# Products on half the partitions, issued alternately, and an attention output product on two column groups

## The chip, the cores and the metric

One core of a Trainium2 chip runs the whole kernel. The metric is device time in microseconds (us); lower is better. The time before is the median of three runs. The trace is of one more execution.

## What is computed

A trunk of two layers over 512 tokens of width 1024. The first layer mixes with sliding-window attention (8 query heads of 64, 2 key heads, window 128, a sink per head) and mLSTM (4 heads, chunks of 128). The second mixes with SSD (8 heads, chunks of 128, 2 groups) and an RWKV-7 recurrence (8 heads of 64). Each mixer is followed by a squared-ReLU MLP of width 4096. Cut to the parts that the change touches:

```python
o = jnp.einsum('bhgnqk,bnkhd->bnqhgd', p.astype(v.dtype), vb)          # attention's output product
qk = jnp.einsum('bnthd,bnshd->bntsh', qc, kc) * w_intra                # mLSTM
a_cum = jnp.cumsum((dt * A.astype(F32)).reshape(bsz, nc, L, G, hg), axis=2)
seg = a_cum[:, :, :, None] - a_cum[:, :, None, :]                      # SSD: every pair of rows in a chunk
decay = jnp.exp(jnp.where(causal, seg, -jnp.inf))
S = S * w_t[:, :, None, :] - sa[..., None] * b_t[:, :, None, :] + v_t[..., None] * k_t[:, :, None, :]   # RWKV-7
```

## The kernel before

Everything is written by hand per engine, with semaphores. The order of TensorE's work is a generator's: `even_front` and `odd_front` mix slots of the input projection (24 one-pass products of 512 columns each: high and low parts of weights and activations, L859 to L861) with the mixers' own small products; `rwkv_chunks` orders the last part of layer 1, where no projection is left to mix in. PSUM has eight banks. `make_plan` hands them out in turn in the order of use: a product may start once the one eight places before it in that order has been drained (`free`), and whoever reads it waits for `full`; `close` signals it.

Weights come by DMA in pieces; ScalarE writes the high part (L1371), GpSimd the low part (L768), and TensorE waits for the low part by `w_cut`. ScalarE cuts a piece only when its place in its queue comes.

The products of the change. Features lie on partitions, two heads of 64 in each block of 128, so a product of one head reads partitions 0 to 63 or 64 to 127 (`par`).

- `score` (L1017): for each of 8 units u, two heads of `par` 0 into one bank, then two of `par` 1 into another; VectorE and ScalarE make the softmax, `att_turn` turns it, and `att_out` (L1028) multiplies it by v two units later. v stands twice side by side (`v_dup`, written by four ScalarE copies, L1533), so that the result of 128 rows by 512 columns holds every head in both halves of the partitions; ScalarE's two drains (L1557) take the right quarter of it each.
- `qk_st` (L1056) and `inter` (L1081) of mLSTM: as the scores, two and two.
- `sub` (L1147): RWKV's blocks for the substitution, for each f four products of `par` 0, then four of `par` 1.
- `a_row` in `ssd_front` (L1168, L1172): for each half, a mask into the whole bank by one product, then four products over 32 partitions that add a row of `a_cum` to it. `a_turned` holds `a_cum` turned, on 32 partitions.
- `mats` (L1232 to L1235): for each of 8 heads four products of 128 columns into a bank, which VectorE masks and copies (`masked`, L2462). For the next chunk the heads' products stand between this chunk's: head 0 before `y`, head 1 before `s_rw` (L1326, L1327), heads 2 to 7 behind it. VectorE masks heads 0 and 1, takes `s_rw` (L2545, L2547), makes the new state (L2550), and masks the other six; `pt` (L1249) of the next chunk waits for all eight. Before the last chunk the turned `y_ssm` go between.

An fp32 product is two instructions in the trace.

Of the kernel before, what the change touches and what calls it, by code (L numbers as in the profile page):

```python
# [34 lines left out]
P = 128  # L35
T = 512
NT = T // P
# [185 lines left out]
def rwkv_chunks():  # L223

    def heads(n, first, last):
        for hh in range(first, last):
            yield "mats", n, hh // 2, hh % 2

    yield from heads(0, 0, 8)
# [4 lines left out]
    for n in range(NT):  # L234
# [53 lines left out]
def make_plan():  # L288
# [11 lines left out]
    for layer in range(2):  # L300
# [38 lines left out]
        else:  # L339
# [27 lines left out]
            for item in rwkv_chunks():  # L367
                put(*item)
# [16 lines left out]
def trunk(nc, dram, out):  # L385
    PLAN = make_plan()
    with ExitStack() as ctx:
# [182 lines left out]
        v_dup = take(NT + 1, 2, P)  # L570
# [90 lines left out]
        acum = tiny(2, 32)  # L661
# [174 lines left out]
        def _(pe):  # L836
# [141 lines left out]
            def even():  # L978
                dup = even_const("dup").rearrange("p (g m) -> p g m", g=2)
                turned = 0  # L980
                for item in even_front():
# [23 lines left out]
                    elif kind == "score":  # L1005
# [7 lines left out]
                        for par in range(2):  # L1013
                            o = free(pe, "score", u, par)
                            r = slice(64 * par, 64 * par + 64)
                            for a in range(2):
                                ins = mm(o[:, a * 256:(a + 1) * 256], q_rot[r, 2 * g + a, n * P:(n + 1) * P],  # L1017
                                         k_dup[r, g, n * P:n * P + 256], start=True, stop=True)
                            close(ins, "score", u, par)
# [30 lines left out]
                for n in range(NT):  # L1050
                    tok = slice(n * P, (n + 1) * P)
                    for par in range(2):
                        o = free(pe, "qk_st", n, par)
                        r = slice(64 * par, 64 * par + 64)
                        for a in range(2):
                            ins = mm(o[:, a * P:(a + 1) * P], conv_out[r, 2 + a, tok], conv_out[r, a, tok],  # L1056
                                     start=True, stop=True)
                        close(ins, "qk_st", n, par)
# [16 lines left out]
                    if n:  # L1075
                        pe.wait_ge(S["c_ready"], n)
                        for par in range(2):
                            o = free(pe, "inter", n, par)
                            r = slice(64 * par, 64 * par + 64)
                            for a in range(2):  # L1080
                                ins = mm(o[:, a * 129:(a + 1) * 129], conv_out[r, a, tok], c_state[r, n, a, :],  # L1081
# [1513 lines left out]
```

## Time and profile before

| | |
|---|---|
| median of 3 runs | 1432.07 us (1429.0 to 1435.8) |
| profiled execution: its time | 1429.38 us |
| its span, first to last instruction | 1427.5 us |
| granted TensorE clock, mean | 0.970 |
| TensorE busy | 1352.4 us (95%) |
| GpSimd, VectorE, ScalarE busy | 657.1, 582.6, 535.6 us |

Busy time says how long an engine has at least one instruction at work. The chain follows the work that ended last back from the end. In a timeline a row may merge several instructions of a line; its second column reaches from the first one's start to the last one's end.

### The profile page before, as it was taken

How to read it: one execution, taken by the hardware profiler on the slowest of the kernel's cores; microseconds unless marked ns; L12 is line 12 of the kernel's file. 1: busy time of each engine (PE TensorE's matmuls, PEld its weight loads, DVE VectorE, ACT ScalarE, POOL GpSimd, SP SyncE). 2: the span in 40 equal slices, each digit the busy share in tenths (PEclk: the TensorE clock that was granted, in tenths of full speed). 3: DMA queues.
4: the chain of work that ended last, by engine and by line, in shares of the span. 5: the costliest groups of instructions: out<-in, count | busy, mean ns of one | idle time of the engine just before them, and what ended most of it. 6: DMA issues, size and time to landing. Idle time of an engine off the chain costs nothing.

```text
span 1427.5 us, 17763 instructions
## 1 busy us (share of the span) xinstructions
PE 1352.4 (95%) x6427; PEld 1085.4 (76%) x6427; DVE 582.6 (41%) x957; ACT 535.6 (38%) x871; POOL 657.1 (46%) x810
## 2 busy tenths in 40 slices
PE   5999968999999999999798999998999999999998
PEld 4777656788888888887477777888878888888886
DVE  4537667421221212345588567365442122121233
ACT  5345653341322413436553424533333132232332
POOL 4653213564554555664234432311365555564562
PEclk9999978999999999999899999999899999999999
DMA  8322101333323323332212211000133333323321
GB/s 271 89 74 60 60 1 31 103 89 91 102 89 89 102 88 93 98 89 74 59 45 67 79 48 30 1 2 1 45 89 90 103 89 92 100 88 95 97 89 59
DMA packets 198034, 109.12 MB, mean 76 GB/s; under 512 B 4570, under 2 KB 195280, under 8 KB 197840
## 3 DMA queue, kind: packets, MB, share of 16 engines
q1 hardware_dynamic: 197552, 108.16, 26.0%
q8 instruction: 43, 0.70, 0.2%
q14 instruction: 23, 0.19, 0.0%
q0 software_dynamic: 416, 0.07, 0.0%
HBM read 106.11 MB, written 2.10 MB: 76 GB/s over the span
## 4 chain that ended last, share of the span: by engine, by line
PE 73%; DVE 7%; ACT 3%; issue 2%; POOL 0%; DVEq 0%; ACTq 0%; POOLq 0%
PE ps L859 20%; PE ps L860 20%; PE ps L861 20%; PE ps L846 1%; PE ps L900 1%; PE ps L901 1%; PE ps L902 1%; DVE late L2462 1%; PE ps L1263 1%; PE ps L1274 1%; PE ps L1252 1%; PE ps L1137 1%; PE ps L1249 0%; PE ps L1317 0%; DVE arena L2533 0%
## 5 line engine op out<-in xcount | busy, mean ns | idle before, releaser
L768 POOL TENSOR_TENSOR w_lo<-raw_w,w_hi 128x256 fp32r<-128x256 f32 x760 | 613.3, 839 | 632.8 <-ACT w_hi L1371 632.8
L1371 ACT ACTIVATE w_hi<-raw_w 128x1024 fp32r<-128x1024 f32 x190 | 201.1, 1058 | 559.0 <-PE ps L861 441.0
L859 PE MATMUL ps<-hn_hi,w_hi 128*128 128x512 f32 x880 | 360.1, 409 | 9.6 <-POOL w_lo L768 8.8
L860 PE MATMUL ps<-hn_lo,w_hi 128*128 128x512 f32 x880 | 351.7, 400 | 0.0
L861 PE MATMUL ps<-hn_hi,w_lo 128*128 128x512 f32 x880 | 351.5, 399 | 0.0
L859 PE MATMUL ps<-hid_hi,w_hi 128*128 128x512 f32 x576 | 228.4, 397 | 0.0
L861 PE MATMUL ps<-hid_hi,w_lo 128*128 128x512 f32 x576 | 228.4, 396 | 0.0
L860 PE MATMUL ps<-hid_lo,w_hi 128*128 128x512 f32 x576 | 228.3, 396 | 0.0
L859 PEld LDWEIGHTS ps<-hn_hi,w_hi 128*128 128x128 f32 x880 | 167.6, 190 | 59.6 <-issue 17.9
L860 PEld LDWEIGHTS ps<-hn_lo,w_hi 128*128 128x128 f32 x880 | 167.9, 191 | 42.2 <-issue 3.1
L861 PEld LDWEIGHTS ps<-hn_hi,w_lo 128*128 128x128 f32 x880 | 167.6, 190 | 41.0
L1892 DVE TENSOR_TENSOR h<-h,ps 128x512 f32<-128x512 f32 x64 | 44.0, 688 | 259.2 <-PE ps L861 259.2
L859 PEld LDWEIGHTS ps<-hid_hi,w_hi 128*128 128x128 f32 x576 | 108.5, 188 | 26.4
L861 PEld LDWEIGHTS ps<-hid_hi,w_lo 128*128 128x128 f32 x576 | 108.5, 188 | 26.5
L860 PEld LDWEIGHTS ps<-hid_lo,w_hi 128*128 128x128 f32 x576 | 108.5, 188 | 26.4
L1881 DVE SCALAR_TENSOR_TENSOR relu<-ps,rms 128x512 f32<-128x512 f32 x64 | 44.3, 692 | 161.5 <-PE ps L861 160.7
L1884 DVE TENSOR_TENSOR hid_lo<-relu,hid_hi 128x512 fp32r<-128x512 f32 x64 | 53.7, 840 | 102.2 <-ACT hid_hi L1442 102.2
L1365 ACT ACTIVATE arena<-ps 128x512 f32<-128x512 f32 (+1 forms) x42 | 23.0, 575 | 56.2 <-PE ps L1317 23.2
L1440 ACT ACTIVATE relu<-relu 128x512 f32<-128x512 f32 x64 | 39.4, 616 | 10.0 <-DVE relu L1881 10.0
L1442 ACT ACTIVATE hid_hi<-relu 128x512 fp32r<-128x512 f32 x64 | 40.5, 633 | 2.0
L1365 ACT ACTIVATE rwkv_raw<-ps 128x512 f32<-128x512 f32 (+1 forms) x29 | 15.2, 540 | 50.4 <-PE ps L861 41.7
L2230 DVE TENSOR_TENSOR relu<-ps,rms 128x512 f32<-128x512 f32 x22 | 15.0, 684 | 40.2 <-PE ps L861 39.8
(371 smaller groups left out, 1444.5 us busy)
## 6 DMA issues: line engine op xcount, KB each, us to landing
raw_w<-in_w_up SPq DMA_DIRECT2D x64, 512.0 KB, 4.0
raw_w<-in_w_down SPq DMA_DIRECT2D x64, 512.0 KB, 3.6
raw_w<-in_o_w_in SPq DMA_DIRECT2D x27, 512.0 KB, 3.8
raw_w<-in_e_w_in SPq DMA_DIRECT2D x19, 512.0 KB, 3.8
raw_w<-in_e_w_out SPq DMA_DIRECT2D x8, 512.0 KB, 3.6
raw_w<-in_o_w_out SPq DMA_DIRECT2D x8, 512.0 KB, 3.5
rwkv_raw<-in_x SPq DMA_DIRECT2D x4, 512.0 KB, 8.4
out<-arena SPq DMA_DIRECT2D x8, 256.0 KB, 2.9
```

Source lines behind the costliest of these rows:

```text
L768: nc.gpsimd.tensor_tensor(w_lo[:, n % CUT, ks], raw_w[:, n % RING, ks], w_hi[:, n % CUT, ks].bitcast(F32), ALU.subtract).then_inc(w_cut, 1)
L859: mm(o, a_hi, b_hi, start=(k == 0), stop=False)
L860: mm(o, a_hi, b_lo, start=False, stop=False)
L861: ins = mm(o, a_lo, b_hi, start=False, stop=(k == KT - 1))
L1365: A(dst, o if src is None else src, ACT.Copy, scale=scale).then_inc(free_sem(*key), 1)
L1371: A(w_hi[:, n % CUT], raw_w[:, n % RING], ACT.Copy).then_inc(w_high, 1)
L1440: A(relu_t[:, j % 2, :], relu_t[:, j % 2, :], ACT.Square).then_inc(hid_square, 1)
L1442: A(hid_hi[:, j, :], relu_t[:, j % 2, :], ACT.Copy).then_inc(hid_high, 1)
L1881: V.scalar_tensor_tensor(out=relu_t[:, j % 2, :], in0=ps[:, b, :], scalar=0.0, in1=rms_t, op0=ALU.max, op1=ALU.mult).then_inc(bank_free[b], 1)
L1884: V.tensor_tensor(hid_lo[:, j, :], relu_t[:, j % 2, :], hid_hi[:, j, :].bitcast(F32), ALU.subtract).then_inc(hid_ready, 1)
L1892: V.tensor_tensor(h[:, j, :], h[:, j, :], ps[:, b, :], ALU.add).then_inc(bank_free[b], 1)
L2230: V.tensor_tensor(stage[:, i % 2, 3:3 + T], o, rms_t, ALU.mult).then_inc(free_sem(*key), 1)
```

## The change

The products that read half the partitions are issued in alternation: one of the lower half, one of the upper, each half into its own bank. That holds for `score`, `qk_st`, `inter`, `sub` and `mats`; `rwkv_chunks` now hands out `mats` by pairs of heads, the first pair before `y`. `a_row` needs the turned `a_cum` on partitions 0 to 31 and again on 32 to 63, so `a_cum` is made twice (one product more, `acum` of three parts) and turned with 64 columns; both masks go first, then the small products of the two halves in alternation. `att_out` keeps v once (`v_kept`) and makes the two `par` as products of 64 output rows each, into partitions 0 to 63 and 64 to 127 of one bank, so that one ScalarE drain takes both.

```diff
-    def heads(n, first, last):
-        for hh in range(first, last):
-            yield "mats", n, hh // 2, hh % 2
+    def pairs(n, first, last):
+        for f in range(first, last):
+            yield "mats", n, f
...
         if more:
-            yield from heads(n + 1, 0, 1)
+            yield from pairs(n + 1, 0, 1)
         yield "y", n
         if more:
-            yield from heads(n + 1, 1, 2)
             yield "s_rw", n
-            yield from heads(n + 1, 2, 8)
+            yield from pairs(n + 1, 1, 4)
...
-        v_dup = take(NT + 1, 2, P)
+        v_kept = take(NT + 1, 2, 64)
...
-        acum = tiny(2, 32)
+        acum = tiny(3, 32)
...
-                        for par in range(2):
-                            o = free(pe, "score", u, par)
-                            r = slice(64 * par, 64 * par + 64)
-                            for a in range(2):
-                                ins = mm(o[:, a * 256:(a + 1) * 256], q_rot[r, 2 * g + a, n * P:(n + 1) * P],
+                        o = [free(pe, "score", u, par) for par in range(2)]
+                        for a in range(2):
+                            for par in range(2):
+                                r = slice(64 * par, 64 * par + 64)
+                                ins = mm(o[par][:, a * 256:(a + 1) * 256], q_rot[r, 2 * g + a, n * P:(n + 1) * P],
                                          k_dup[r, g, n * P:n * P + 256], start=True, stop=True)
...
-                            ins = mm(o, v_dup[:, n + blk, g, :], att_pt[:, u % 2, blk, :],
-                                     start=(blk == 0), stop=(blk == 1))
+                            for par in range(2):
+                                ins = mm(o[64 * par:64 * par + 64, 0:256], v_kept[:, n + blk, g, :],
+                                         att_pt[:, u % 2, blk, par * 256:(par + 1) * 256],
+                                         start=(blk == 0), stop=(blk == 1))
...
-                        mm(o[:, 0:32], upper, da_, start=True, stop=True)
-                        close(mm(o[:, 32:64], ones, da_, start=True, stop=True), "a_cum")
+                        for twin in range(2):
+                            mm(o[:, 32 * twin:32 * twin + 32], upper, da_, start=True, stop=True)
+                        close(mm(o[:, 64:96], ones, da_, start=True, stop=True), "a_cum")
...
-                        for par in range(2):
-                            r = slice(64 * par, 64 * par + 64)
-                            o = free(pe, "sub", f, par)
-                            for t in range(NT):
-                                c = slice(t * P, (t + 1) * P)
-                                ins = mm(o[:, c], kk_s[r, f, c], b_s[r, f, c], start=True, stop=True)
-                            close(ins, "sub", f, par)
+                        o = [free(pe, "sub", f, par) for par in range(2)]
+                        for t in range(NT):
+                            c = slice(t * P, (t + 1) * P)
+                            for par in range(2):
+                                r = slice(64 * par, 64 * par + 64)
+                                ins = mm(o[par][:, c], kk_s[r, f, c], b_s[r, f, c], start=True, stop=True)
+                                if t == NT - 1:
+                                    close(ins, "sub", f, par)
...
+                        o = [free(pe, "a_row", n, half) for half in range(2)]
                         for half in range(2):
-                            o = free(pe, "a_row", n, half)
-                            mm(o.rearrange("p (a t) -> p a t", a=4), mask_r[:, 0:P], over(mask_r[:, P:2 * P], 1, 4),
-                               start=True, stop=False, skip_group_check=True)
-                            for j in range(4):
-                                c = 8 * n + 4 * half + j
-                                ins = mm(o[:, j * P:(j + 1) * P], ident[0:32, c:c + 1].to_broadcast([32, P]),
-                                         a_turned[0:32, :], start=False, stop=True, skip_group_check=True)
-                            close(ins, "a_row", n, half)
+                            mm(o[half].rearrange("p (a t) -> p a t", a=4), mask_r[:, 0:P],
+                               over(mask_r[:, P:2 * P], 1, 4), start=True, stop=False, skip_group_check=True)
+                        for j in range(4):
+                            for half in range(2):
+                                r = slice(32 * half, 32 * half + 32)
+                                c = 32 * half + 8 * n + 4 * half + j
+                                ins = mm(o[half][:, j * P:(j + 1) * P], ident[r, c:c + 1].to_broadcast([32, P]),
+                                         a_turned[r, :], start=False, stop=True, skip_group_check=True)
+                                if j == 3:
+                                    close(ins, "a_row", n, half)
...
-                    for par in range(2):
-                        r = slice(64 * par, 64 * par + 64)
-                        ins = A(y_mix[r, 2 * g:2 * g + 2, n * P:(n + 1) * P],
-                                o[r, par * 256:par * 256 + 256].rearrange("p (a t) -> p a t", a=2), ACT.Copy)
-                    ins.then_inc(free_sem("att", u), 1)
+                    A(y_mix[:, 2 * g:2 * g + 2, n * P:(n + 1) * P], o[:, 0:256].rearrange("p (a t) -> p a t", a=2),
+                      ACT.Copy).then_inc(free_sem("att", u), 1)
```

`qk_st`, `inter` and `mats` are rewritten in the same way; the four copies of v are one.

TensorE, in `rwkv_chunks`, from the end of `y` (L1315, L1317) of chunk 0 over `s_rw` (L1326, L1327); before:

```order
L1315 MATMUL ps<-rwkv_raw,late 128x64
L1317 MATMUL ps<-arena,late 128x64
L1232 MATMUL ps<-arena 128x128
L1233 MATMUL ps<-arena,rwkv_raw 128x128
L1234 MATMUL ps<-rwkv_raw 128x128
L1235 MATMUL ps<-rwkv_raw,arena 128x128
L1326 MATMUL ps<-rwkv_raw,arena 128x128
L1327 MATMUL ps<-arena 128x128
```

The same place now (`y` is L1330 and L1332, `s_rw` L1341 and L1342, `mats` L1248):

```order
L1330 MATMUL ps<-rwkv_raw,late 128x64
L1332 MATMUL ps<-arena,late 128x64
L1341 MATMUL ps<-rwkv_raw,arena 128x128
L1342 MATMUL ps<-arena 128x128
L1341 MATMUL ps<-rwkv_raw,arena 128x128
L1342 MATMUL ps<-arena 128x128
L1341 MATMUL ps<-rwkv_raw,arena 128x128
L1342 MATMUL ps<-arena 128x128
L1341 MATMUL ps<-rwkv_raw,arena 128x128
L1342 MATMUL ps<-arena 128x128
L1248 MATMUL ps<-arena 128x128 x2
L1248 MATMUL ps<-arena,rwkv_raw 128x128 x2
```

Head 1's four products have gone from between `y` and `s_rw` to before `y`; the other heads follow `s_rw` in pairs.

TensorE, in `ssd_front` of chunk 0, between b's turns (L846) and `cb` (L1177); before:

```order
L846 MATMUL ps<-main,arena 128x128 x2
L1168 MATMUL ps<-mask_r 128x512
L1172 MATMUL ps<-arena,main 128x128 x4
L1168 MATMUL ps<-mask_r 128x512
L1172 MATMUL ps<-arena,main 128x128 x4
L1177 MATMUL ps<-arena 128x128 x2
```

And now:

```order
L849 MATMUL ps<-main,arena 128x128 x2
L1178 MATMUL ps<-mask_r 128x512 x2
L1184 MATMUL ps<-arena,main 128x128 x8
L1190 MATMUL ps<-arena 128x128 x2
```

The second mask stands directly behind the first, and the eight small products are in one row.

## Rows read from the trace of the kernel before

**Rows 1.** The page: PE's busy time, and the chain's shares by engine.

```profile
PE 1352.4 (95%) x6427; PEld 1085.4 (76%) x6427; DVE 582.6 (41%) x957; ACT 535.6 (38%) x871; POOL 657.1 (46%) x810
...
PE 73%; DVE 7%; ACT 3%; issue 2%; POOL 0%; DVEq 0%; ACTq 0%; POOLq 0%
```

**Rows 2.** Busy time by stage: stretch, its length, busy time (instructions) by engine, clock.

```profile
95.00:175.00 80.00, 78.95 (x372) 56.59 (x371) 53.84 (x110) 45.25 (x119) 27.05 (x36) 1.00 0.20 60
...
875.00:1002.00 127.00, 112.83 (x936) 104.17 (x936) 62.64 (x115) 52.33 (x103) 25.14 (x22) 0.94 0.00 1
```

**Rows 3.** Timeline of PE, LoRA products: start, length, engine, line, shape [idle before].

```profile
656.72 0.69 PE L1114 MATMUL ps<-rwkv_raw,lora 64*128 64x512 f32 x1
656.72 0.69 PE L1116 MATMUL ps<-rwkv_raw,lora 64*128 64x512 f32 x1
```

**Rows 4.** Timeline of PE, scores of one unit and what follows.

```profile
118.59 1.14 PE L1017 MATMUL ps<-arena,rwkv_raw 64*128 64x256 f32 x8
119.67 0.33 PE L846 MATMUL ps<-main,rwkv_raw 128*128 128x128 f32 x1
```

**Rows 5.** Timeline of PE, one attention output product and what follows.

```profile
129.60 1.88 PE L1028 MATMUL ps<-y_mix,arena 128*128 128x512 f32 x4
131.32 0.59 PE L1042 MATMUL ps<-arena,main 128*128 128x512 f32 x1
```

**Rows 6.** Timeline of PE, a_row of chunk 1 and what follows.

```profile
816.89 0.48 PE L1168 MATMUL ps<-mask_r 128*128 128x512 f32 x1
817.30 1.15 PE L1172 MATMUL ps<-arena,main 32*128 32x128 f32 x8
818.39 0.50 PE L1168 MATMUL ps<-mask_r 128*128 128x512 f32 x1
...
819.90 0.71 PE L1177 MATMUL ps<-arena 128*128 128x128 f32 x4
```

**Rows 7.** Timeline of ScalarE and of VectorE, end of attention.

```profile
178.58 0.77 ACT L1557 ACTIVATE y_mix<-ps 64x256 f32<-64x256 f32 x2 [0.46 <-PE ps L1028]
...
188.21 2.20 DVE L2101 SCALAR_TENSOR_TENSOR arena<-rwkv_raw,small 128x128 f32<-128x128 f32 x8 [4.64 <-ACT rwkv_raw L1365]
```

**Rows 8.** Timeline of PE, sub of f = 0, projections, and the wait behind f = 3.

```profile
716.60 1.71 PE L1147 MATMUL ps<-arena 64*128 64x128 f32 x16
718.24 0.50 PE L859 MATMUL ps<-hn_hi,w_hi 128*128 128x512 f32 x1
718.58 0.40 PE L860 MATMUL ps<-hn_lo,w_hi 128*128 128x512 f32 x1
718.81 0.40 PE L861 MATMUL ps<-hn_hi,w_lo 128*128 128x512 f32 x1
...
742.74 0.47 PE L859 MATMUL ps<-hn_hi,w_hi 128*128 128x512 f32 x1 [2.61 <-POOL w_lo L768]
```

**Rows 9.** The chain (start, length, what), before the RWKV chunks.

```profile
874.47 0.70 DVE late L2462
```

**Rows 10.** Timeline of PE and of VectorE, from y to s_rw of chunk 0.

```profile
907.70 0.48 PE L1232 MATMUL ps<-arena 64*128 64x128 f32 x2
...
908.79 0.49 PE L1326 MATMUL ps<-rwkv_raw,arena 128*128 128x128 f32 x2
...
910.87 0.69 DVE L2547 COPY arena<-ps 128x512 f32<-128x512 f32 x1 [1.29 <-PE ps L1327]
```

**Rows 11.** The chain in chunk 1, the group norm.

```profile
934.67 6.29 DVE arena L2533 x6
```

**Rows 12.** Timeline of VectorE between chunks 2 and 3.

```profile
975.60 3.68 DVE L2462 SCALAR_TENSOR_TENSOR late<-ps,main 128x512 f32<-128x512 f32 x6 [0.15 <-DVE arena L2550]
979.67 1.53 DVE L1848 TENSOR_TENSOR hid_lo<-ps,hid_hi 128x512 fp32r<-128x512 f32 x2 [0.40 <-ACT hid_hi L1783]
```

**Rows 13.** PE by stretch, before and in pt: length, busy (count), granted clock, DMA.

```profile
914.70:917.30 2.60, 0.00 (x0) 1.00 0.00 0
917.40:920.80 3.40, 3.40 (x17) 0.50 0.00 0
```

More of the change, by code:

```diff
@@ L367, in make_plan @@
             for item in rwkv_chunks():
-                put(*item)
+                if item[0] == "mats":
+                    put(*item, 0)
+                    put(*item, 1)
+                else:
+                    put(*item)
             put_mixed(1, "y_rw")
@@ L1051, in even @@
                     tok = slice(n * P, (n + 1) * P)
-                    for par in range(2):
-                        o = free(pe, "qk_st", n, par)
-                        r = slice(64 * par, 64 * par + 64)
-                        for a in range(2):
-                            ins = mm(o[:, a * P:(a + 1) * P], conv_out[r, 2 + a, tok], conv_out[r, a, tok],
+                    o = [free(pe, "qk_st", n, par) for par in range(2)]
+                    for a in range(2):
+                        for par in range(2):
+                            r = slice(64 * par, 64 * par + 64)
+                            ins = mm(o[par][:, a * P:(a + 1) * P], conv_out[r, 2 + a, tok], conv_out[r, a, tok],
                                      start=True, stop=True)
-                        close(ins, "qk_st", n, par)
+                            if a:
+                                close(ins, "qk_st", n, par)
                     if n < NT - 1:
@@ L1076, in even @@
                         pe.wait_ge(S["c_ready"], n)
-                        for par in range(2):
-                            o = free(pe, "inter", n, par)
-                            r = slice(64 * par, 64 * par + 64)
-                            for a in range(2):
-                                ins = mm(o[:, a * 129:(a + 1) * 129], conv_out[r, a, tok], c_state[r, n, a, :],
+                        o = [free(pe, "inter", n, par) for par in range(2)]
+                        for a in range(2):
+                            for par in range(2):
+                                r = slice(64 * par, 64 * par + 64)
+                                ins = mm(o[par][:, a * 129:(a + 1) * 129], conv_out[r, a, tok], c_state[r, n, a, :],
                                          start=True, stop=True)
-                            close(ins, "inter", n, par)
+                                if a:
+                                    close(ins, "inter", n, par)
                 for j in range(3):
@@ L1226, in odd @@
                     elif kind == "mats":
-                        f, par = item[2], item[3]
-                        r = slice(64 * par, 64 * par + 64)
+                        f = item[2]
                         if n == 0:
                             pe.wait_ge(S["tilde"], f + 1)
-                        o = free(pe, *item)
-                        mm(o[:, 0:P], kk_s[r, f, tok], b_s[r, f, tok], start=True, stop=True)
-                        mm(o[:, P:2 * P], raw[r, 4 + f, rtok], kk_s[r, f, tok], start=True, stop=True)
-                        mm(o[:, 2 * P:3 * P], raw[r, 4 + f, rtok], raw[r, f, rtok], start=True, stop=True)
-                        close(mm(o[:, 3 * P:4 * P], b_s[r, f, tok], raw[r, f, rtok], start=True, stop=True), *item)
+                        o = [free(pe, *item, par) for par in range(2)]
+                        kk_, b_, r_, k_ = kk_s[:, f, tok], b_s[:, f, tok], raw[:, f, rtok], raw[:, 4 + f, rtok]
+                        for i, (left, right) in enumerate(((kk_, b_), (k_, kk_), (k_, r_), (b_, r_))):
+                            for par in range(2):
+                                r = slice(64 * par, 64 * par + 64)
+                                ins = mm(o[par][:, i * P:(i + 1) * P], left[r], right[r], start=True, stop=True)
+                                if i == 3:
+                                    close(ins, *item, par)
                     elif kind == "pt":
```

28 lines of the change are left out of this document (12 added, 16 removed).

## The prediction

> **What bounds the kernel now.** I read the page's busy shares and chain first, to see which engine sets the end; then busy time by stage, to see where the tensor engine (PE) still waits; then the timeline of PE round each product that the change touches, to price it; last the chain and the timelines of the other engines behind it, to see who waits for it. PE is busy for 95% of the span and makes 73% of the chain [rows 1]. In the stretch of the attention products PE is busy for 78.95 of 80 us; in the last stretch, the RWKV chunks, for 112.83 of 127 us [rows 2]. So time saved on PE should count almost whole in the first and only in part in the last.
>
> An fp32 product stands in the trace as two instructions. Two products on different halves of the partitions can run side by side here: the LoRA pair (rows 0 to 63, rows 64 to 127) starts twice at 656.72 [rows 3]. The reader should look next at the scores: eight instructions of 256 columns start at 118.59, and the next work starts at 119.67 [rows 4]. One instruction of 512 columns over all 128 rows takes (131.32 - 129.60) / 4 = 0.43 us [rows 5], so one of 256 takes 0.215, eight in a row 1.72. They took 1.08: the scores already overlap, although they are issued half after half, since a half has only four instructions. Alternation brings something only where more than four stand in a half, or where the halves were one.
>
> **The change, part by part.**
>
> Scores, and mLSTM's qk_st and inter: four instructions in a half, as above. I count 0. If their order gained something it could be the part of 1.08 that is not 4 x 0.215, 0.22 each; if it hurt, as much. Both ends go to the range.
>
> Attention's output product (8 of them): before, four instructions over 128 columns of weights and 512 moving columns, 1.72 us [rows 5]. Now eight of 64 by 256, in two column groups. No row shows two column groups at once. One end: they pair as the halves of rows do, 4 x 0.215 = 0.86, plus the 0.22 that the scores pay over their own steps [rows 4], plus 0.1 for entering (from the mask's start to the first a_row product is 0.41 [rows 6]; a one-pass product of 512 columns steps by 0.23, 718.58 to 718.81 [rows 8], so the switch is 0.2 at most). That is 1.18 to 1.28, a gain of about 0.5 each. Other end: no pairing, 8 x 0.215 + 0.3 = 2.05, a loss of about 0.33 each. I take the first, since the nearest rows, split by rows, pair fully. The first four products (u = 0 to 3) lie before the last score, where PE hardly waits: 4 x 0.5 = 2.0. The fifth is lost in a wait for the softmax. Behind it ScalarE sets the end: its two drains of 0.38 (0.77 for the pair, at 178.58) start after a wait for PE, and it then works without a break until VectorE, idle for 4.64 us, starts at 188.21 [rows 7]. The change makes one drain of each pair, three times: 3 x 0.38 = 1.1, and the sixth product is ready 0.5 sooner: 1.6. Together **3.6**. Without pairing: -4 x 0.33, and on ScalarE about -0.3, so **-1.6**. The copies of v (four to one) lie under projections, 0.
>
> Behind that, mLSTM's chain runs on VectorE and begins at 188.21, so it moves with it. The span has no other cover there.
>
> a_cum gets one more product of 32 columns and its drain 32 more columns; a_turn turns 64 columns. All lie beside a VectorE chain or under the projections: below 0.2 us, 0.
>
> sub (16, 32 and 16 instructions): 16 take 718.24 - 716.60 = 1.64 us. Paired fully it would be 8 x 0.11 + 0.3 = 1.2; all three about 1.6 together. But the chain goes over VectorE's key parts and ScalarE's sub_blocks to the next weights' cut, and PE waits 2.61 us for that until 742.74 [rows 8]. PE arrives sooner and waits longer: **0**, at most 1.6.
>
> a_row (4 chunks): before, from the first mask at 816.89 to the next product at 819.90, 3.01 us: each half its own mask, with a switch between, and 8 small instructions [rows 6]. Now both masks (0.23 + 0.41 to the first small one) and two rows of eight side by side, as long as one was, 818.39 - 817.30 = 1.09. Sum 1.73, gain **1.28**. The chain runs over PE in chunks 0, 1 and 2. In chunk 3 the chain is VectorE's own queue, down to the masked drain at 874.47 [rows 9], and the gain is covered. 3 x 1.28 = **3.8**. If 32-row groups did not pair, only the saved switch is left, 0.3 each.
>
> mats (the RWKV products): chunk 0's 64 instructions wait for that same drain at 874.47 [rows 9]: 0. In chunks 1 to 3 one pair now stands ahead of y, and s_rw directly behind y. The pair costs y nothing new, since its second half runs beside the first. Between y and s_rw 908.79 - 907.70 = 1.09 us go away, and VectorE waits for s_rw there (910.87) [rows 10]: **1.1**. Into chunk 2 VectorE is held by the group norm until 934.67 + 6.29 = 940.96 [rows 11]; and has two masked drains of 0.61 ahead of s_rw, which is there by then: 0. Into chunk 3, PE's turns of y_ssm stand behind all mats, ScalarE behind them, and VectorE at 979.67 behind ScalarE [rows 12]. The mats end 1.1 sooner by the order and about 0.9 by pairing (48 instructions, 3.8 us from 910.87 [rows 10] to the idle at 914.7 [rows 13], would take 24 x 0.11 + 0.3 = 2.9), but VectorE's own masked drains (3.68 from 975.60) end at 979.3 - 1.1, so the work at 979.67 starts at 978.2: **1.5**. Banks come round eight by eight; those that the new order needs are drained by then. RWKV: **2.6**.
>
> Sum: 3.6 + 3.8 + 2.6 = **10.0 us**. Against the profiled execution, 1429.38, that is 1419.4; it lies 2.7 under the median of the runs, 1432.07, against which I predict **1422.0**.
>
> The page "TensorE: Matmul & The Clock Gate" of the Trainium skill, section "Part 3: Packing small matmuls — row/col tiling", has a rule against this change: a weight load overlaps running products only when its row group differs, and two column groups share all their rows. By the rows it does not hold as it stands, since the 0.43 us steps of four products on the same rows [rows 5] are two passes of at most 0.23 each, with no room for a load. By that rule the sum would be some 5 us instead of 10.
>
> **The rivals.**
>
> (a) Column groups do not gain: they take turns, or their loads are laid bare. For it: no row shows them paired. Against it: the rows' halves pair. For laid-bare loads the price is at most 0.1 for each of eight, the part of a switch seen in [rows 6], and ends near the same place. Gain -1.6 + 3.8 + 2.6 = 4.8: 1427.3, within 0.5%.
>
> (b) The change does not pair a_row's 32-row groups, while all else holds: 10.0 - 3 x 1.0 = 7.0, 1425.
>
> (c) The clock. PE stood idle from 914.7 to 917.3 and then had 0.50 of its clock, the 1.2 GHz level, until 920.8 [rows 13]; 3.4 us at half speed cost 1.7. PE will now wait longer before each chunk (2.6 becomes 3.5 to 4.7) and behind y_ssm, where the clock stayed whole. Three more such stretches cost 5: 1427.
>
> (d) Slower than before: switching to column groups costs far more than switching rows, at every instruction instead of every product. The gains outside attention are 6.4, and ScalarE's saved drains 1.1. It decides once a product takes over 1.0 us more than before; with a switch of 0.2 at each of eight instructions and no pairing, 8 x 0.415 = 3.3, it is 1.6 more, eight times 13 us: 1432.07 + 13 - 7.5 = 1437.6. Against it: row groups pay once a product [rows 4].
>
> (e) More comes through: sub's 1.6, 0.22 from scores, a stretch at half clock that goes: 1418.
>
> **How the numbers follow.** Forecast 0.51; (a) 0.22, of which by the skill's rule 0.05; (b) 0.06; (c) 0.09; (d) 0.04; (e) 0.08. Runs of before span 1429.0 to 1435.8, and a measurement can tell about 0.5%, 7.2 us, from nothing. The forecast's 10 is beyond that with some 8 in 10, (e) always, (b) half of the time, the others no: faster 0.53, same 0.42, slower 0.05. The range takes in (a), (b), (c) and (e) with 2 us of spread: 1416 to 1429.5.
>
> **What would show it.** Right: the output product's line, eight instructions a product, with next work about 1.2 us after its first; a_row's piece about 1.7 us; s_rw's first product directly behind y; PE's wait near 742 grown from 2.6 towards 4.2; scores at 1.08 as before; span near 1417.5. Wrong: output products of 2 us, a_row's piece over 2.5, or new stretches at 0.50 of the clock behind the longer waits.

## The result, and the profile after

The change ran in two sets, each beside the kernel before:

| | median, us | range | runs | ratio to before, 95% interval |
|---|---|---|---|---|
| before, first set | 1431.86 | 1429.0 to 1435.8 | 4 | |
| before, second set | 1435.98 | 1429.1 to 1436.8 | 17 | |
| change, first set | 1417.71 | 1411.8 to 1419.5 | 4 | 0.9887 [0.9862, 0.9911] |
| change, second set | 1411.85 | 1411.7 to 1414.4 | 5 | 0.9847 [0.9829, 0.9865] |

So it is faster by 1.1 to 1.5%: 16 to 22 us, where the forecast was 10. The stated range began at 1416.0; against the 1432.07 that the forecast started from, the two ratios give 1415.9 and 1410.2. Three of the four runs of the first set have a mean granted clock of 0.966 or 0.967, all five of the second 0.972 or 0.973. The profiled execution of the first set took 1419.52 us (span 1417.7), the slowest of its four, while that of before, 1429.38, was among the fastest of its own: the two traces differ by only 9.8. That matters below, since the traces alone would have confirmed the sum.

The page of the change, where it answers to [rows 1]. PE is busy for 17 us less:

```profile
PE 1335.1 (94%) x6461; PEld 1072.1 (76%) x6461; DVE 582.6 (41%) x957; ACT 530.9 (37%) x860; POOL 657.2 (46%) x810
...
PE 71%; DVE 9%; ACT 3%; issue 2%; POOL 0%; DVEq 0%; ACTq 0%; POOLq 0%
```

The timeline of PE in the change: scores, an output product and the row behind it [rows 4, 5], a_row of chunk 0 [rows 6]:

```profile
126.94 1.14 PE L1020 MATMUL ps<-arena,rwkv_raw 64*128 64x256 f32 x8
128.01 0.55 PE L849 MATMUL ps<-main,rwkv_raw 128*128 128x128 f32 x3
...
129.03 1.08 PE L1033 MATMUL ps<-y_mix,arena 128*64 128x256 f32 x8
130.04 0.70 PE L1048 MATMUL ps<-arena,main 128*128 128x512 f32 x1
...
794.47 0.70 PE L1178 MATMUL ps<-mask_r 128*128 128x512 f32 x2
795.10 1.16 PE L1184 MATMUL ps<-arena,main 32*128 32x128 f32 x16
796.19 0.71 PE L1190 MATMUL ps<-arena 128*128 128x128 f32 x4
```

Scores stay at 1.07 us. From the output product's first instruction to the next work it is 1.01 us (before 1.72), so two column groups run side by side: eight instructions of 256 columns in the time of 4.7 single ones of 0.215. The neighbours pay for it. The step into the product is 0.20 instead of 0.11, and the row behind it lasts 0.70 instead of 0.59 [rows 5]. PE's lead over the kernel before grows by 0.5 with each of the first four products, so the 1.2 that I took was right with the two switches in it. The page "TensorE: Matmul & The Clock Gate" of the Trainium skill, section "Part 3: Packing small matmuls — row/col tiling", lets a weight load overlap running products only where the row groups differ. This trace does not bear that out: the product's eight loads, all on the same rows, lie between 129.03 and 129.66, under its instructions from 129.03 to 130.11. The table of the same section of the Trainium skill lists a measured gain for packed columns, 2.38 times for three tiles; the trace agrees in direction, and the prediction had weighed the rule alone. A_row takes 1.72 us for 3.01: 1.29 less, as predicted.

The timeline of ScalarE, then of VectorE, at the end of attention [rows 7]: one drain each time, and VectorE starts at 184.41 instead of 188.21:

```profile
181.76 0.38 ACT L1567 ACTIVATE y_mix<-ps 128x256 f32<-128x256 f32 x1 [0.31 <-PE ps L1033]
...
184.41 2.20 DVE L2110 SCALAR_TENSOR_TENSOR arena<-rwkv_raw,small 128x128 f32<-128x128 f32 x8 [2.99 <-ACT rwkv_raw L1380]
```

PE's own timeline at the places where it now stands longer: the weights' cut [rows 8], the fourth pair of chunk 0, and `pt` of chunk 2, the product that waits for all eight masked drains ("the masks' product" in what follows):

```profile
739.42 0.47 PE L862 MATMUL ps<-hn_hi,w_hi 128*128 128x512 f32 x1 [3.59 <-POOL w_lo L771]
...
863.57 0.80 PE L1248 MATMUL ps<-arena 64*128 64x128 f32 x4 [2.43 <-DVE arena L2421]
...
938.96 1.41 PE L1264 MATMUL ps<-late 128*128 128x128 f32 x5 [4.72 <-DVE late L2471]
```

The first is the predicted absorption of sub. The second was not foreseen: a pair needs both of its banks before its first product, and the fourth pair's are freed late. Counted from before to the change, and less the 0.65 us by which the start differed, PE was ahead by 3.2 us behind attention (predicted 3.6) and by 11.0 behind the last a_row; at the end of the RWKV chunks it was 9.1. The a_rows had brought four times 1.27, and 3.2 more, because two stretches at half clock that before has are missing: one directly behind the a_row of chunk 0 (801.4) and one behind short waits, ahead of the a_row of chunk 2 (835.5).

### The profile page after: what moved, and what is told of

Same layout as the page of the kernel before. It is cut to its first block, busy times and chain, and to the rows that moved or that the text cites. A ratio compares the mean times of both kernels' runs of the same rounds, so it can differ in the third digit from the quotient of the medians.

```text
span 1417.7 us, 17835 instructions
## 1 busy us (share of the span) xinstructions
PE 1335.1 (94%) x6461; PEld 1072.1 (76%) x6461; DVE 582.6 (41%) x957; ACT 530.9 (37%) x860; POOL 657.2 (46%) x810
## 4 chain that ended last, share of the span: by engine, by line
PE 71%; DVE 9%; ACT 3%; issue 2%; POOL 0%; DVEq 0%; ACTq 0%; POOLq 0%
PE ps L862 20%; PE ps L863 20%; PE ps L864 20%; PE ps L849 1%; PE ps L903 1%; PE ps L904 1%; PE ps L905 1%; DVE late L2471 1%; DVE arena L2255 1%; PE ps L1278 1%; PE ps L1289 1%; PE ps L1267 1%; PE ps L1146 1%; PE ps L1264 1%; PE ps L1332 0%
## 5 line engine op out<-in xcount | busy, mean ns | idle before, releaser
L1846 DVE TENSOR_TENSOR rms<-rms,relu 128x512 f32<-128x512 f32 x27 | 28.2, 1044 | 7.7 <-ACT relu L1406 7.7
```

The lines of the kernel that those rows point to most:

```text
L1846: V.tensor_tensor(rms_t, rms_t, relu_t[:, k % 2, :], ALU.add).then_inc(summed, 1)
```

## The experiments

**The parts, each alone.** Each kernel is the one before with some of the diff's pieces.

> Of the change only attention's output product on two column groups, v kept once, and one ScalarE drain in place of two. Theory A (the sum as predicted, the parts add): the attention stretch ends 3.6 us sooner and all of it is left at the end: 3.6 us, 0.25% faster than before. Theory B (the sum of the parts is right only after the half-clock stretches are counted: each wait of PE moves or changes one): in the trace of the whole change 3.2 us were left behind attention, with a longer wait of PE at 170 and a half-clock stretch that before does not have; here the same: 3.2 us, and up to 1.7 more or less by a stretch elsewhere. Both: products step by 0.215 us per pair of column groups, next work 1.0 us behind the first. A rival C: the gain that is larger than predicted lies here (the drains and the copies of v free ScalarE more than I counted): 6 us or more.

> Of the change only a_cum, a_turn and a_row: the two halves of a chunk's rows on 32-row groups side by side, both masks first. Theory A: 1.28 us in each of chunks 0, 1 and 2, the fourth covered: 3.8 us, 0.27% faster. Theory B: the same 3 x 1.28, and besides the two half-clock stretches of before at 801.4 and 835.5 go, since PE no longer waits at these places (1.54 and 1.7 us in the trace of the whole change), and the fourth 1.27 is kept at least until the next long wait: 7 us, 0.5% faster. The fourth is covered if the gain from the start of the RWKV chunks to the end is one product's less than at the last a_row.

> Of the change only the RWKV products in pairs, with a pair ahead of y and s_rw directly behind y. Theory A (as predicted): 1.1 us into chunk 1, 1.5 into chunk 3: 2.6 us, 0.18% faster. Theory B (from the trace of the whole change): a pair waits until both of its banks are free, so PE stands at the fourth pair of chunk 0 for 2.4 us and runs the turns behind it at half clock; the later waits of PE are 4.2 to 4.7 us instead of 2.6 and chunk 2 gets a half-clock stretch of 6.8 us instead of 3.4: 0 to 0.6 us slower than before, no gain.

> Of the change only the order within scores, qk_st, inter and sub: instructions alternate between the halves. Theory A: scores, qk_st and inter 0; sub runs about 0.45 us less for each of its products, all of it absorbed by the wait for the next weights' cut at 736 to 742: 0. Theory B: 0 as well at that place, but the wait of PE there grows by 1 us, and a longer wait costs up to one half-clock stretch of 3.4 us, 1.7 us slower. A rival C, that the gain larger than predicted comes from here: 2 us or more faster.

| part alone | median, us | range | ratio to before (1431.89) |
|---|---|---|---|
| attention | 1427.28 | 1423.8 to 1433.1 | 0.9972 [0.9954, 0.9989] |
| a_row | 1420.42 | 1420.2 to 1420.9 | 0.9910 [0.9892, 0.9929] |
| RWKV pairs and order | 1428.35 | 1420.8 to 1430.4 | 0.9961 [0.9945, 0.9977] |
| alternation | 1431.71 | 1428.8 to 1436.0 | 0.9993 [0.9978, 1.0008] |

Attention gave 4.0 us (predicted 3.6; 3.0 by its trace), alternation nothing, as predicted. A_row gave 12.9, over three times its 3.8 and beyond both theories, and its six runs lie within 0.7 us while those of before spread over 8.7 (1428.0 to 1436.8). The cause must be something that makes the runs of before differ. The windows of PE in the RWKV kernel's trace, whose a_row is that of before, show it: stretch and length, busy time (instructions), granted clock.

```profile
815.80:819.15 3.35, 3.35 (x24) 1.00 0.22 70
819.20:822.55 3.35, 3.35 (x10) 0.50 0.24 80
```

The timeline of the same kernel says what PE did in the first of the two:

```profile
815.69 0.48 PE L1171 MATMUL ps<-mask_r 128*128 128x512 f32 x1
816.10 1.15 PE L1175 MATMUL ps<-arena,main 32*128 32x128 f32 x8
817.18 0.50 PE L1171 MATMUL ps<-mask_r 128*128 128x512 f32 x1
817.62 1.15 PE L1175 MATMUL ps<-arena,main 32*128 32x128 f32 x8
818.70 0.80 PE L1180 MATMUL ps<-arena 128*128 128x128 f32 x4
```

PE was busy throughout and had no wait, but most of its products used 32 of 128 rows; then the clock fell to the 1.2 GHz level for one stretch of 3.4 us, which costs 1.7. This trace has another such stretch behind a_row at 843.1, and the kernels of alternation and of the order alone (below) have the same two (819.9 and 843.8, 818.8 and 842.7). The trace of before has none at these two places; it has one behind the a_row at 797.78, without a wait in the piece itself, but PE had waited 0.99 us just ahead of it, until 797.59:

```profile
797.95:801.36 3.41, 3.41 (x24) 1.00 0.62 159
801.40:804.78 3.38, 3.38 (x10) 0.50 0.44 113
```

So where these stretches fall, and how many, differs from run to run of the same work. Counted over the five traces with the a_row of before and no dummy products (before, attention, RWKV, alternation, order), 8 of 20 a_rows have such a stretch directly behind them, and in six of the eight PE had no wait in the 5 us before either; over the four with the new a_row and no dummy products it is 0 of 16. The page "TensorE: Matmul & The Clock Gate" of the Trainium skill, section "HAM oscillation — how this bites in real kernels", puts the fall down to idle gaps of PE. These rows show one with no gap. In rival (c) I looked for stretches only behind waits.

Few rows are not the only such work. All ten traces of kernels without dummy products, the change's too, have one more stretch at half clock with no wait before it, behind 32 products of two columns over all 128 rows (the RWKV bonus, L1155). In that of before, its timeline and windows:

```profile
749.97 3.63 PE L1155 MATMUL ps<-main,arena 128*128 128x2 f32 x32
...
750.15:753.56 3.41, 3.41 (x32) 1.00 0.35 84
753.60:757.00 3.40, 3.40 (x9) 0.50 0.22 66
```

The change leaves these products as they are.

**The clock behind a_row, by itself.** One edit to the kernel before, besides a clearing of the added rows:

```diff
-    ins = mm(o[:, j * P:(j + 1) * P], ident[0:32, c:c + 1].to_broadcast([32, P]),
-             a_turned[0:32, :], start=False, stop=True, skip_group_check=True)
+    ins = mm(o[:, j * P:(j + 1) * P], ident[:, c:c + 1].to_broadcast([P, P]),
+             a_turned, start=False, stop=True, skip_group_check=True)
```

> The kernel before, with one edit: a_row's small products read all 128 rows in place of 32 (the rows added are zeros against zeros, the sum is the same), so their number, columns and order stay, and nothing is paired. Theory A (a_row's gain is its own time, pairing and a saved switch): nothing changes, 1432. Theory B (before, a_row's narrow products lower the clock behind them, where PE has no idle time at all: 801.4 in the trace of before, 819.2 and 843.1 in those of two others; the change removes these stretches besides its own 1.28 us each): with all rows at work the stretches go, a_row's pieces keep 3.0 us each, and 3 to 7 us are gained, with less spread from run to run. Rival C (the clock falls because these products move few columns, not because they use few rows): stretches stay, 1432.

Measured: 1424.12 us (1422.5 to 1427.6), ratio 0.9926 [0.9910, 0.9942], 10.6 us. Its windows, a_row and the stretch behind it, in chunks 0 and 1:

```profile
798.60:801.60 3.00, 3.00 (x25) 1.00 0.68 180
801.60:805.00 3.40, 3.40 (x17) 1.00 0.20 27
815.50:818.30 2.80, 2.80 (x26) 1.00 0.05 12
818.30:821.70 3.40, 3.40 (x17) 1.00 0.41 144
```

No stretch behind any of the four a_rows is left, though the number of columns stayed; rival C falls for these products. One expectation was missed: the pieces did not keep 3.0 us. The timeline:

```profile
815.57 0.48 PE L1168 MATMUL ps<-mask_r 128*128 128x512 f32 x1
815.89 1.05 PE L1172 MATMUL ps<-arena,main 128*128 128x128 f32 x8
816.70 0.47 PE L1168 MATMUL ps<-mask_r 128*128 128x512 f32 x1
817.01 1.05 PE L1172 MATMUL ps<-arena,main 128*128 128x128 f32 x8
817.90 0.61 PE L1177 MATMUL ps<-arena 128*128 128x128 f32 x4
```

That is 2.33 us: 0.81 for eight products' instructions over all rows against 1.08 over 32 rows, and less at each switch. Three times 0.68 is 2.0 us of time of their own; the other 8 or so are the clock. Since the pieces became shorter as well, this run does not tell the number of rows from the length of the narrow work. Traces show only part of those 8: one or two stretches behind a_rows in each kernel that has them, 1.7 to 3.4 us. But nine of the 17 runs of before in this set took 1436 with a mean clock of 0.961 to 0.963, against 0.966 to 0.970 for the eight between 1429 and 1433, and no profile caught such a run. The 12 runs of the RWKV part alone and the 12 of its order alone never go below 0.964, although their a_rows are those of before; so which stretches make a run of 1436 is open.

The mean clocks of all runs give an estimate of the whole. One minus the mean clock, times the span, is the time lost to the clock (some of it in waits, where it costs nothing): 48 us before and 39 with a_row alone, 9 less, of 12.9; in the second set 50 before, 41.5 with a_row over 128 rows and 39 with the whole change. The change is 22 us faster in that set, of which 11 are thus clock and 11 its own, near the predicted 10.

**Do the parts add?** The product of the four ratios is 0.9837, which is 23 us, against 16 in the first set of the change.

> The whole change once more, for its spread and beside its parts. By the parts measured alone (0.9972, 0.9910, 0.9961, 0.9993) the product of the ratios is 0.9837, 23 us; the whole gave 0.9887, 16 us. If the parts add, this run shows 0.984 within its error; if the RWKV pairs lose in the whole change what they gain alone, it stays at 0.9887: about 1416 us.

> The whole change without its RWKV part: mats half after half, one half ahead of y, the next between y and s_rw, as before. Theory A (the parts add): slower than the whole change by the 2.6 us of the prediction, or by the 5 us that this part gave alone. Theory B (in the whole change the pairs give nothing, since a pair stands for both banks at the fourth pair of chunk 0, 2.4 us, and the longer waits bring longer half-clock stretches): the same as the whole change within 1 us, or up to 1 us faster; in the trace no wait of 2.4 us at the fourth pair and none of 4.2 to 4.7 us ahead of the masks.

The change again: 1411.85, ratio 0.9847, which the sum of the parts fits; the first set's 0.9887 lies 7 us off, just outside the joint error, and its clocks were lower. Without its RWKV part: 1422.13 (1416.6 to 1422.3), ratio 0.9901 [0.9882, 0.9921], 7.7 us slower by the ratios with an error of 4 (10.3 by the medians); my theory B fell, and of theory A's two figures the 5 fits and the 2.6 does not. The profile of the second set of the change ran at 1412.46 and that of the first at 1419.52: one kernel, and the same waits before the last u and y, 0.89 us each time at u. The timeline of both, the first set's (984.38), then the second's:

```profile
984.38 2.13 PE L1317 MATMUL ps<-late 128*128 128x64 f32 x16 [0.89 <-ACT late L1380]
```

```profile
983.29 1.97 PE L1317 MATMUL ps<-late 128*128 128x64 f32 x16 [0.89 <-ACT late L1380]
```

And the windows around them, of the first set's run and of the second's:

```profile
982.60:986.00 3.40, 2.51 (x23) 1.00 0.00 0
986.10:999.60 13.50, 12.75 (x52) 0.50 0.00 1
```

```profile
981.50:985.00 3.50, 2.61 (x25) 1.00 0.00 0
985.00:998.60 13.60, 12.85 (x78) 1.00 0.00 1
```

One falls to half clock for 13.7 us there, the other not at all, which is most of the 7 us between the two runs. All other profiles of kernels without dummy products have a stretch of 10 to 14 us at half clock there.

The order of the RWKV part alone (two heads ahead of y, s_rw directly behind it, no pairs):

```diff
-            yield from heads(n + 1, 0, 1)
+            yield from heads(n + 1, 0, 2)
         yield "y", n
         if more:
-            yield from heads(n + 1, 1, 2)
             yield "s_rw", n
```

> The kernel before with the order of the RWKV part alone: two heads of the next chunk ahead of y and s_rw directly behind y, each half still by itself, no pairs. Theory A (prediction: the order gives 1.1 us into chunk 1 and 1.1 of the 1.5 into chunk 3, but the second head ahead of y now takes the time that pairing would have saved, about 0.5 each chunk): 1 us. Theory B (the order is what the RWKV part gives, the pairs themselves nothing, since their time is lost in waits): as much as the RWKV part alone gave, 5 us by the ratio. Rival C (the pairs give it): 0.

Measured: 1429.30 (1425.6 to 1433.3), ratio 0.9979 [0.9959, 0.9999], 3.0 us; the intervals of order alone and of the whole RWKV part (5.6) overlap, so this did not tell A from B. In the traces s_rw's sum on VectorE came 1.2 us sooner with pairs and 0.6 with the order alone, counted from the masks' product of chunk 0; at the masks' product of chunk 1, 0.6 and 0.5 were left.

**Holding the clock up.** Dummy products (they compute nothing that is needed) into a bank that is about to be overwritten, issued where PE would wait. The helper and one of the places:

```diff
+def fill(o, count, wide=T):
+    for _ in range(count):
+        mm(o[:, 0:wide], ones, const("reset")[:, 0:wide], start=True, stop=True)
...
+    if level == 0 and half == 0 and n:
+        fill(free(pe, *item), (4, 5, 1)[n - 1])
```

> The whole change, with dummy products added where PE waits: 512 columns of ones against a constant, about 0.43 us each, into a bank that the next real product overwrites from its start; some 110 in all, about as many in each wait as fit in it. They compute nothing that is needed. Clock theory: the half-clock stretches behind these waits go, in the attention stretch, at 735 to 790 and in the RWKV chunks, and 10 to 20 us are gained against the whole change: 1397 to 1407 us. Rival: the fills end later than the waits and cost what they bring, or the stretches come whatever PE does: 1416 to 1425 us.

> The whole change with dummy products in the RWKV waits alone, half as many as in the run with all fills, where each turned out to take 0.86 us instead of 0.43 and to end behind the wait: four, five and one ahead of the masks' products of chunks 1 to 3, three and one at the other waits. They compute nothing that is needed. Clock theory: the half-clock stretches behind these waits go (10 to 17 us in length in the traces, half of it time, of which a part is hidden behind VectorE): 2 to 5 us faster than the whole change, 1407 to 1410. Rival: most of what a full clock gives there ends in the next wait for VectorE: the same as the whole change.

> The whole change with dummy products in all longer waits, half as many as in the first try: at the waits of attention and mLSTM, ahead of kk_inv, in two projections that wait for their weights' cut, and in the RWKV chunks. They compute nothing that is needed and now end inside the waits. Clock theory: granted clock 0.985 or more and, with no overrun, 10 to 15 us faster than the whole change: 1398 to 1403. Rival (overrun was not what cost the first try; full clock on stretches where VectorE or ScalarE is late gives only longer waits): 1410 to 1415.

> As the run before it, and besides two dummy products ahead of the third y_diag (a wait of 2.03 us) and one of 384 and one of 256 columns in the two short waits ahead of the last u and y (0.89 and 0.75 us), behind which one trace of the whole change has 13.7 us at half clock and the other, with the same waits, has none. Clock theory: the late stretch is gone in every run; up to 7 us faster than the run before it where that one has the stretch, and runs closer together. Rival: no change, or 1 us slower by overrun.

| the change, with fills | median, us | range | clock | ratio to before |
|---|---|---|---|---|
| all, twice too many | 1428.65 | 1422.9 to 1434.1 | 0.986 to 0.994 | 0.9965 [0.9948, 0.9983] |
| RWKV waits alone | 1413.51 | 1411.3 to 1415.0 | 0.971 to 0.973 | 0.9858 [0.9832, 0.9885] |
| all | 1408.71 | 1404.7 to 1412.3 | 0.983 to 0.989 | 0.9832 [0.9807, 0.9857] |
| all, and three more places | 1401.94 | 1399.4 to 1403.1 | 0.990 to 0.995 | 0.9779 [0.9752, 0.9805] |

The first kept the clock but made PE late everywhere: I had taken 0.43 us for a dummy, which is one of its two instructions. A full clock is thus no gain by itself. Fills in the RWKV waits alone changed nothing that can be told, against my 2 to 5. All waits with half as many, ratio 0.9832, can't be told from the change without fills, 0.9847, either, against my 10 to 15. Only with the three more places, the last u and y among them, is the kernel clearly faster: 0.9779, 0.9793 and 0.9806 in three sets, 6 to 10 us less than the change. Windows by stage, first of the change, then of it with all fills and the three places: the clock rises from 0.94, 0.82, 0.85 and 0.88 to 1.00, 0.97, 0.94 and 1.00; only from 780 to 860, where nearly nothing is filled, it falls, from 1.00 to 0.96.

```profile
120.00:200.00 80.00, 70.90 (x401) 0.94 0.13 40
200.00:260.00 60.00, 49.08 (x213) 0.82 0.15 45
690.00:780.00 90.00, 75.31 (x329) 0.85 0.22 59
780.00:860.00 80.00, 77.66 (x455) 1.00 0.23 67
860.00:1002.00 142.00, 121.27 (x1005) 0.88 0.02 5
```

```profile
120.00:200.00 80.00, 75.07 (x426) 1.00 0.13 40
200.00:260.00 60.00, 56.82 (x243) 0.97 0.16 45
690.00:780.00 90.00, 87.68 (x393) 0.94 0.22 59
780.00:860.00 80.00, 74.87 (x427) 0.96 0.21 63
860.00:1002.00 142.00, 136.67 (x1098) 1.00 0.04 11
```

**Before and change at equal clock.** What the change has of its own should be left when the clock is up in both.

> The kernel before with the same dummy products in its waits as the last run (they compute nothing that is needed). Clock theory: the stretches of before behind waits go, those behind a_row's narrow products stay: 10 to 15 us faster than before, 1417 to 1422, and 15 to 20 slower than the change with fills. Rival (fills help only the changed kernel): 1430.

> The same, and a_row's products over 128 rows, so that the clock stays up behind them as well. Theory A (all that the prediction missed is the clock): the change with fills is faster than this by the predicted 10 us, at equal clock: about 1412. Theory B (terms of the sum were too small besides): the difference stays 15 us or more, 1417. Rival C (terms too large): 5 us or less, 1407.

> The change with all fills once more, on the same chip as the two kernels of before that it is compared with: 1402, clock 0.99.

> The change with all fills, but the RWKV part as before. Theory A (the RWKV part has 2.6 us of its own): 1404 to 1405. Theory B (what it gave without fills was only the place at which half-clock stretches fell): 1402. Theory C (it has the 5 to 8 us that the ratios gave): 1407 to 1410.

Measured: before with fills 1421.65 (1419.0 to 1422.1), ratio 0.9936 [0.9924, 0.9948]; with a_row over 128 rows besides 1416.48, 0.9903 [0.9888, 0.9917]; the change with fills 1401.36, 0.9793 [0.9779, 0.9807]; without its RWKV part 1407.02, 0.9835 [0.9821, 0.9849]. Widening the rows gave 4.7 us here, where the waits are filled, against 10.6 without fills. The 15 us between the second and the third speak for theory B. But the fills had been sized for the change's waits. The timeline of the kernel with fills and without the RWKV part, ahead of chunk 2's masks' products, of PE and then of VectorE's masked drains:

```profile
935.93 4.56 PE L844 MATMUL ps<-main 128*128 128x512 f32 x10
940.33 1.84 PE L1279 MATMUL ps<-late 128*128 128x128 f32 x15
```

```profile
935.78 2.47 DVE L2492 SCALAR_TENSOR_TENSOR late<-ps,main 128x512 f32<-128x512 f32 x4
```

The drains end at 938.25, the dummies hold PE until 940.33. In the change with fills the masks' product starts 0.36 us behind its last drain; here it is 1.72 later than that, and 0.86 in the chunk before. So 2.6 of the 15 us are the experiment's own fault. With three and three in place of four and five:

> The kernel before with all fills and a_row's products over 128 rows, but three and three dummy products ahead of the masks' products of chunks 1 and 2 in place of four and five, so that they end before VectorE's masked drains. Theory A (what the prediction missed is the clock, its own terms are right): 2.6 us faster than with four and five, 1413 to 1414, and 10 to 12 slower than the change with fills. Theory B (the RWKV part has the whole 5 us of its own): as before, 1416 to 1417, 15 slower.

> The change with all fills, for the comparison on the same chip: 1401 to 1402.

Measured: 1413.73 (1412.1 to 1415.5), ratio 0.9879 [0.9856, 0.9903], and 1404.01 (1401.6 to 1408.4), ratio 0.9806 [0.9780, 0.9833]: 9.7 us between them in this set. The loss by the fills is as theory A had it. By the prediction's terms this pair should differ by 8.0 rather than 10, since 0.68 of each of three a_rows is in both. The traces of the pair differ by 5.1 us only: that of the change with fills is the slowest of its five runs and has the lower clock, 0.986 against 0.989, so even this pair is not at quite the same clock. Stage by stage, from these traces, where the RWKV stretch is at full clock in both: the RWKV stretch, from its first product to the projection behind it, takes 126.80 and 124.45 us, so its part has 2.35 of its own (predicted 2.6). In these traces and in those of the pair before them, attention and mLSTM left 5.1 (predicted 3.6), with the 0.2 and 0.4 by which the starts differ counted in; one stretch of 3.4 us at half clock more in the slower of each pair is part of it. A_row has 0.6 a chunk left against the widened one (2.33 to 1.72), its other 0.68 being in both. The intervals of the two ratios leave 10 us an error of about 5, so this says "near 10", no more.

## Why the prediction was wrong, point by point

- **Direction and the mechanisms of the products: right.** Column groups pair (0.5 us gained for each product, as predicted), 32-row groups pair (1.72 for 1.73), scores stay as they were, s_rw stands directly behind y, sub's gain ends in the next wait (2.61 to 3.59 us). Rivals (a), (b) and (d) fell. (In the unpaired case 8 x 0.215 + 0.3 is 2.02 and not 2.05; it changes nothing.)
- **Attention, 3.6: about right.** 3.0 to 3.2 by traces, 4.0 by the ratio; 5.1 with the clock held up. In the first trace of the change PE's wait at 170 grew (1.78 to 2.35 us) and a half-clock stretch at 173.7 took some of it back.
- **A_row, 3.8: the step that failed.** Its own time was right: 1.27 in each of four chunks, the fourth covered. What the term left out is the clock behind it, which it put at nothing. Before, 8 of 20 a_rows had a stretch of 3.4 us at half clock directly behind them, in a stretch of projections where PE is the bound; behind the shorter piece there is none. The run with this part alone gave 12.9 us, 9 more than the term (6 to 12 by the interval), and the estimate from the mean clocks is also 9. Widening the rows alone gave 10.6, of which about 8 clock. The stretches seen in traces make 1.7 to 3.4 of the 9; where the rest falls was not seen.
- **RWKV, 2.6: right in size at full clock (2.35), too small for the clock as it is.** The trace with this part alone has 1.1 in the RWKV stretch (0.6 into chunk 1, where I had 1.1); the ratio says 5.6. The excess goes with the clock: the RWKV kernel's runs at 1420.8, 1425.4 and 1430 have mean clocks of 0.975, 0.971 and 0.966. Which stretch the fast runs lack was not seen for this kernel, as its only trace is of a run at 1430; the 13.7 us one at 986 is a candidate. Why this part makes such runs more frequent was not settled. The wait of the fourth pair for both banks was overlooked. By itself it costs nothing: from the first mats to the masks' product of chunk 0 PE's lead falls by 1.55 us in the second trace of the change, and by 1.53 without pairs. In the first trace it falls by 2.76, with 6.8 us at half clock right behind that wait.
- **Rival (c)** had the clock with the wrong sign and for waits only; **rival (e)** held "a stretch at half clock that goes", a single one, inside 4 us for everything, with a chance of 0.08.
- **The range.** The sum was set against one profiled execution and moved by 2.7 us to the median, as if a run's place were noise. The executions of before, 1429 to 1436, were already the sign that a term varied by 7 us from run to run, which a change to PE's work could switch off. The low end, 1416.0, had room for 2 us of it. That the two first traces differ by about the predicted 10 is luck: the slowest run of the change stands there beside a fast one of before.

## What to carry to other kernels

Where runs of one kernel differ by more than a timing's jitter and the granted clock differs with them, list every stretch at half clock and what PE did right before it, products on few rows included, not its waits alone. In this kernel narrow products in the middle of work that PE bounds cost more than their time, and pairing them or spreading them over all rows took that away. Where the waits themselves can't go, a few dummy products that end before the wait does gave another 6 to 10 us here; twice as many made it 17 slower than none, so size them by what one takes in the trace.

## What the hardware showed that was not expected

- The clock fell to half behind work in which PE was busy throughout, with most products on 32 of 128 rows (8 of 20 times). With the same products on 128 rows it stayed. It also fell behind 3.6 us of two-column products over all rows.
- Sixteen instructions of 128 columns over 32 rows took 2 x 1.08 us, over 128 rows 2 x 0.81, in the same places.
- The same 0.89 and 0.75 us waits were followed by 13.7 us at half clock in one run and by none in another.
- Two column groups of 64 run fully side by side in fp32: 0.216 us for each pair of 256-column instructions. Going in and out cost the neighbouring rows 0.2 us a product.
